# Eight weight jobs of the first gate moved from the dense attention loop into the Fourier stage

## The chip, the cores and the metric

The kernel runs on one core of a Trainium2 chip. The metric is the device time of one execution in microseconds (us). Its engines are named as the profile names them: PE (TensorE, matmuls; PEld its weight loads), DVE (VectorE), ACT (ScalarE), POOL (GpSimd), SP (SyncE, which issues the weight transfers here).

## What is computed

The reference is a network of two layers of one kind and a third block of another kind, on 512 tokens of width 1024. The change touches the mixers of the two layers alone:

```python
u = rmsnorm(x, g_mix[l])
p = u @ w_in[l]                       # 1024 Fourier columns, 3 x 384, 2 x 512, 512
y_a = fourier_mix(a_in) @ w_br_a[l]   # real part of a 2-D DFT over tokens and the 128 channels of each of 8 groups
y_b = dilated_mixture(qb, kb, vb, rel_bias[:, :6]) @ w_br_b[l]   # 3 pairs of heads, weighted by shares
y_c = diff_attention(qc, kc, vc, ...) @ w_br_c[l]                # 4 heads, a = p0 - lam * p1, 512 x 512 scores
gates = sigmoid(u @ w_gate[l] + b_gate[l]).reshape(..., 3, D)
merged = gates[0] * y_a + gates[1] * y_b + gates[2] * y_c
x = x + merged @ w_out[l]
```

## The kernel before, in words

All activations are held transposed: 128 channels of a tile on the partitions, 512 tokens along the free axis; 1024 channels are 8 tiles. Every product with a weight matrix is cut into **jobs**. A job is one 128 x 1024 slab of weights (512 KB, one row of `jobs` in DRAM) and gives one output tile of 128 x 512 in a PSUM bank. For precision each operand is split into a high part, rounded to fp32r, and a low part, so `product` (L429) issues three matmuls for each of 8 input tiles, 24 of 512 columns in all (L436 to L438), over `w_hi`, `w_lo` and the activations' `hi` and `lo`.

Weights pass through two slots, `s` = 0 and 1. SP loads `raw[:, s]` (L388) when POOL has made the slot's previous `w_lo`; ACT's `pump(s)` (L942) copies `raw` to `w_hi` in two halves, the first as soon as the job before it in the slot is half done, the second when it is done; POOL makes `w_lo = raw - w_hi` (L401). All jobs of the program are in one list that `arrays_of` builds (L2124), and jobs with even places use slot 0. So the order of jobs on PE is the order in the list, and PE, ACT, DVE and the list have to agree. Job s gives bank `ps[s]`; DVE's `scaled` (L1460) reads it out times `rs`, the reciprocal norm, and signals `evac[s]`, for which the next job in the bank waits.

Each engine has its own program, in order, with semaphores between the engines; `Count` keeps the values. In a layer the mixers go: 18 jobs of `w_in`; three dilated groups with 12 jobs between their steps; `dilated_rows`; `fourier`; `mix_groups`; `dense`; 8 jobs of the two other branch products; 14 of the other gates; 8 of `w_out`.

**Fourier stage** (PE L467, ACT L1020, DVE L1502). For each of 8 groups PE does the transform along the channels of the next group (`along_channels`, L471, from the folded inputs in `pt`, into ps2 or ps3), for groups 1 to 4 the transposes of a value tile for the later dense stage (L487), and the transform along the tokens (L493 to L499) in two banks: p with the cosines (ps4 or ps0), q with the sines (ps5 or ps1). ACT copies z (L1028) and q (L1037); DVE combines p and q in four operations to y (L1537 to L1540), ACT makes `m_hi` of it (L1039) and DVE `m_lo` (L1544): the activations of the branch product with `w_br_a`. No weight job runs in this stage, since the banks 0 and 1 hold q and p. Beside it DVE computes the shares of the dilated groups on two partitions (`dilated_rows`, `dilated_shares`, L1580 to L1601), and ACT their exponential (`mix_exp`, L1066).

**mix_groups** (PE L570, DVE L1603). The shares are spread to 128 partitions by a matmul with `sel` (L574, ps7), once for each of three dilated groups, and DVE multiplies and adds to `pt[:, MIX]`. It stands ahead of the first logits on DVE, through `hf` and T5 as temporaries.

**Dense loop** (PE L578, ACT L1070, DVE L1614). Sixteen rounds u, each 128 queries of one head, in a pipeline that is two rounds deep. PE in round u: scores of round u+2 (L586, two matmuls of 64 rows into ps2 and ps3, after the logits have freed them), wait for the probabilities, four transposes (L599, ps4), **one job** (L602, L604), wait for ACT's copy of the transposed tile (L1084), four PV matmuls (L609, ps5). DVE: `probabilities(u)` (L1635 to L1638), then what belongs to a job, then `logits(u+2)` (two operations L1624, a reduction L1628), which waits for the transposes of round u, since it overwrites their source. ACT: the copy, the gate's function and pump, the exponentials of round u+2 (L1076), the copies of PV (L1093, L1094).

Even rounds run a job of the first gate (`u_hi`, slot 0), which DVE scales into T7 and ACT puts through the sigmoid (L1086); odd rounds one of `w_br_a` (`m_hi`, slot 1), and DVE multiplies gate and product into `pt[:, u // 2 - 1]` one round later (L1654). So the two kinds alternate in the list.

Of the kernel before, what the change touches and what calls it, by code (L numbers as in the profile page):

```python
# [10 lines left out]
ALU = mybir.AluOpType  # L11
# [4 lines left out]
P = 128  # L16
S = 512
D = 1024
# [195 lines left out]
def build(nc, jobs, x_in, small_in, mem_in, pos_in, rel_in, lam_in, dft_in, hot_in, eye_in, sel_in,  # L214
          window_in, chunk_in, swap_in, rows8_in, out):
    NJ = jobs.shape[0]
    with ExitStack() as ctx:
# [64 lines left out]
        OC = 8  # L282
        MIX = 12
        YB, YC = 8, 16
        dft_c, dft_s = tab[:, 0:P], tab[:, P:2 * P]
# [130 lines left out]
        def _(pe):  # L416
# [50 lines left out]
            def fourier():  # L467
# [13 lines left out]
                for g in range(8):  # L481
                    if g < 7:
                        along_channels(g + 1)
                    if 1 <= g <= 4:
                        pe.wait_ge(vt_done, c.take("vt_done"))
                        for r in range(4):
                            mm = pe.transpose(ps[6][:, r * P:r * P + P], pt[:, VC + g - 1, r * P:r * P + P], ident)  # L487
                        mm.then_inc(vt_full, c.up("vt_full"))
                    z = T[:, g % 2].rearrange("p (t n) -> p t n", t=4)
                    pe.wait_ge(z_act, c.now("z_act") - (1 if g < 7 else 0))  # L490
                    pe.wait_ge(y_done, c.take("y_done") - 1)
                    p, q = ps[4 if g % 2 == 0 else 0], ps[5 if g % 2 == 0 else 1]
                    pe.matmul(p[:, 0:EVEN], z[:, 0], cos_even, start=True, stop=False)  # L493
                    if g == 0:
                        pe.wait_ge(middle_copied, c.next("middle"))
                    pe.matmul(p[:, 0:EVEN], middle, middle_of[:, g], start=False, stop=True)
                    pe.matmul(p[:, EVEN:HALF], z[:, 1], cos_odd, start=True, stop=True)
                    pe.matmul(q[:, 0:EVEN], z[:, 2], sin_even, start=True, stop=True)
                    pe.matmul(q[:, EVEN:HALF], z[:, 3], sin_odd, start=True, stop=True).then_inc(pq_full, c.up("pq"))  # L499

# [68 lines left out]

            def mix_groups(first_scores):  # L570
                pe.wait_ge(mixw_done, c.next("mixw"))
                for g in range(3):
                    pe.wait_ge(wb_free, c.take("wb_free"))
                    pe.matmul(ps[7][:, :], sel[:, :], rows_m[:, g], start=True, stop=True).then_inc(wb_full, c.up("wb_full"))  # L574
                    if g == 0:
                        first_scores()

            def dense():  # L578
# [9 lines left out]

                mix_groups(lambda: scores(0))
                pe.wait_ge(vt_done, c.now("vt_done"))  # L590
                scores(1)
                for u in range(16):
# [7 lines left out]
                    mm.then_inc(tr_full, c.up("tr_full"))  # L600
                    if u % 2 == 0:
                        job(0, u_hi, u_lo)  # L602
                    else:
                        job(1, m_hi, m_lo, ready=(m_ready, c.now("m")) if u == 1 else None)  # L604
                    pe.wait_ge(tr_copied, c.now("tr_copied"))
# [329 lines left out]
        def _(act):  # L935
# [84 lines left out]
            def fourier():  # L1020
# [3 lines left out]
                for g in range(8):  # L1024
                    act.wait_ge(z_full, c.next("z_full"))
                    if g >= 2:
                        act.wait_ge(pq_full, c.now("pq"))
                    act.activation(T[:, g % 2], ps[2 + g % 2][:, :], ACT.Copy).then_inc(z_act, c.up("z_act"))  # L1028
                    if g == 2:
                        mix_exp()  # L1030
                    if g:
                        fourier_out(g - 1)
                fourier_out(7)

            def fourier_out(g):
                act.wait_ge(pq_full, c.next("pq"))
                act.activation(T[:, 4 + 2 * (g % 2), 0:HALF], ps[5 if g % 2 == 0 else 1][:, 0:HALF], ACT.Copy).then_inc(q_copied, c.up("q_copied"))  # L1037
                act.wait_ge(y_done, c.next("y_done"))
# [31 lines left out]
            def dense():  # L1070
# [11 lines left out]
                for u in range(16):  # L1082
                    act.wait_ge(tr_full, c.next("tr_full"))
                    act.activation(T[:, 4 + u % 2], ps[4][:, :], ACT.Copy).then_inc(tr_copied, c.up("tr_copied"))  # L1084
                    if u % 2:
                        gate(T[:, 7], T[:, 7], 0, ACT.Sigmoid, bgate(0, u // 2))  # L1086
                    pump(1 - u % 2)
                    if u % 2:
                        skip(1)
                    if u < 14:  # L1090
# [336 lines left out]
        def _(dve):  # L1427
# [74 lines left out]
            def fourier():  # L1502
                for g in range(8):
                    if g:
                        fourier_out(g - 1)
                    if g > 1:
# [4 lines left out]
                    if g == 1:  # L1511
                        dilated_rows()
                    if g >= 4:
                        dilated_shares(g - 4)
                fourier_out(7)
# [15 lines left out]
            def fourier_out(g):  # L1531
                dve.wait_ge(q_copied, c.next("q_copied"))
                c.up("pq")
                if g > 1:
                    dve.wait_ge(m_ready, c.now("m"))
                y, p, q = T[:, 7 if g % 2 == 0 else 3], ps[4 if g % 2 == 0 else 0], T[:, 4 + 2 * (g % 2)]
                dve.tensor_tensor(y[:, 0:HALF:2], p[:, 0:EVEN], q[:, 0:EVEN], ALU.subtract)  # L1537
                dve.tensor_tensor(y[:, S - 2:HALF - 1:-2], p[:, 1:P], q[:, 1:P], ALU.add)
                dve.tensor_tensor(y[:, 1:HALF - 1:2], p[:, EVEN:HALF], q[:, EVEN:HALF], ALU.subtract)
                dve.tensor_tensor(y[:, S - 1:HALF - 1:-2], p[:, EVEN:HALF], q[:, EVEN:HALF], ALU.add).then_inc(y_done, c.up("y_done"))  # L1540

# [60 lines left out]

            def mix_groups():  # L1603
                for g in range(3):
                    dve.wait_ge(wb_full, c.next("wb_full"))
                    dst = hf if g == 0 else T[:, 5]
                    dve.tensor_tensor(dst, pt[:, QB + g], ps[7][:, :], ALU.mult).then_inc(wb_free, c.up("wb_free"))
                    dve.wait_ge(wb_free, c.now("wb_free"))
                    if g == 1:
                        step(dve.tensor_tensor(hf, hf, T[:, 5], ALU.add))  # L1610
                    if g == 2:
                        step(dve.tensor_tensor(pt[:, MIX], hf, T[:, 5], ALU.add))

            def dense():  # L1614
# [28 lines left out]
                for u in range(17):  # L1643
                    if u < 16:
                        probabilities(u)
                        c.up("tr_full")
                    if u % 2:
                        if u > 1:
                            dve.wait_ge(evac[1], c.now("evac1"))
                        scaled(0, T[:, 7])  # L1650
                    elif u:
                        dve.wait_ge(silu_done, c.next("silu"))
                        dve.wait_ge(job_done[1], c.next("job1"))
                        dve.tensor_tensor(pt[:, u // 2 - 1], T[:, 7], ps[1][:, :], ALU.mult).then_inc(evac[1], c.up("evac1"))  # L1654
                    if u < 14:
# [14 lines left out]
            def mixers():  # L1670
# [17 lines left out]
                fourier()  # L1688
                mix_groups()
                dense()  # L1690
# [433 lines left out]
def arrays_of(i):  # L2124

    jobs = []
    for l in range(LAYERS):
# [3 lines left out]
        jobs += [weight_jobs(i["w_in"][l]), np.zeros((1, P, D), np.float32)]  # L2131
        jobs.append(np.stack([a[0], weight_jobs(i["w_br_a"][l])], 1).reshape(-1, P, D))
        gates = np.stack([a[1], a[2]], 1).reshape(-1, P, D)
# [59 lines left out]
```

## Time and profile before

| | |
|---|---|
| three runs, median | 3734.37 us |
| lowest, highest | 3733.26, 3742.38 us |
| the profiled execution, its own time | 3740.04 us |
| its span in the trace | 3738.3 us |
| mean granted clock of PE | 0.967 |
| PE busy | 3511.4 us, 94% of the span |
| DVE, ACT, POOL busy | 1597.6, 1380.8, 1481.7 us |
| DMA | 309.08 MB, mean 83 GB/s |

The span is the time from the first to the last instruction in the trace; the execution's own time is 1.7 us longer. All times of rows are us from the span's start, from this one execution. The granted clock is a share of full speed, 2.4 GHz; 0.50 is 1.2 GHz. A fp32 matmul shows as two instructions, and ends of matmuls are modelled, so I read distances between starts.

### The profile page before, as it was taken

Reading aid. Unit: us, or ns where it says so; the run is one execution under the profiler, and the core shown is the slowest. Engines: PE = TensorE matmul, PEld = TensorE weight load, DVE = VectorE, ACT = ScalarE, POOL = GpSimd, SP = SyncE. Lnnn points to the kernel's source line nnn. Section 1 sums busy time; section 2 is a strip of 40 time slices with the busy share of each in tenths; the row PEclk is TensorE's granted clock in tenths of the full one; section 3 lists DMA queues with packets and bytes.
Section 4 is the critical chain, followed back from the end, with each engine's and each line's share of the span. In section 5 each row is a group of like instructions: output and inputs, shape, how many; then the busy total and the mean of one; then the engine's idle time right before and its main releaser. Section 6 shows DMA issues by size and latency. Waiting matters only on the chain.

```text
span 3738.3 us, 50030 instructions
## 1 busy us (share of the span) xinstructions
PE 3511.4 (94%) x16516; PEld 2872.7 (77%) x16516; DVE 1597.6 (43%) x2302; ACT 1380.8 (37%) x2387; POOL 1481.7 (40%) x1124
## 2 busy tenths in 40 slices
PE   8999998999999999999989999998897987889997
PEld 6888885778888888878757888886677886558886
DVE  4223525644322432244275442324786665243224
ACT  4223323644322432242346342324463233233222
POOL 4445431354444554454213544444220024224443
PEclk9999998999999999999989999999998998989998
DMA  3223321222222222232112322222120012113222
GB/s 113 98 98 101 116 73 38 69 96 95 96 97 100 97 101 99 97 122 95 57 44 73 107 94 97 96 95 90 51 74 9 10 40 90 45 51 100 97 95 90
DMA packets 87302, 309.08 MB, mean 83 GB/s; under 512 B 9823, under 2 KB 11873, under 8 KB 87060
## 3 DMA queue, kind: packets, MB, share of 16 engines
q1 hardware_dynamic: 82512, 297.96, 23.8%
q10 hardware_dynamic: 4676, 9.62, 0.9%
q8 instruction: 70, 1.15, 0.1%
q14 instruction: 44, 0.36, 0.0%
HBM read 305.36 MB, written 2.17 MB: 82 GB/s over the span
## 4 chain that ended last, share of the span: by engine, by line
PE 88%; DVE 7%; ACT 2%; issue 2%; ACTq 0%; DMA 0%; POOL 0%; DVEq 0%; POOLq 0%; SPq 0%
PE ps L436 26%; PE ps L438 25%; PE ps L437 25%; PE ps L846 1%; PE ps L586 1%; PE ps L855 1%; PE ps L609 1%; PE ps L849 1%; PE ps L916 1%; PE ps L599 1%; PE ps L524 0%; PE ps L755 0%; PE ps L901 0%; DVE x L1733 0%; PE ps L734 0%
## 5 line engine op out<-in xcount | busy, mean ns | idle before, releaser
L401 POOL TENSOR_TENSOR w_lo<-raw,w_hi 128x512 fp32r<-128x512 f32 x1120 | 1481.5, 1328 | 2227.5 <-ACT w_hi L946 1754.3
L436 PE MATMUL ps<-u_hi,w_hi 128*128 128x512 f32 (+1 forms) x2990 | 1177.1, 394 | 36.2 <-DVE u_lo L1722 16.4
L437 PE MATMUL ps<-u_hi,w_lo 128*128 128x512 f32 (+1 forms) x2990 | 1158.0, 387 | 0.0
L438 PE MATMUL ps<-u_lo,w_hi 128*128 128x512 f32 (+1 forms) x2990 | 1157.7, 387 | 0.0
L436 PEld LDWEIGHTS ps<-u_hi,w_hi 128*128 128x128 f32 x2990 | 568.1, 190 | 165.1 <-issue 36.2
L437 PEld LDWEIGHTS ps<-u_hi,w_lo 128*128 128x128 f32 x2990 | 568.0, 190 | 115.4 <-issue 5.8
L438 PEld LDWEIGHTS ps<-u_lo,w_hi 128*128 128x128 f32 x2990 | 567.3, 190 | 114.4
L948 ACT ACTIVATE w_hi<-raw 128x512 fp32r<-128x512 f32 x560 | 352.4, 629 | 764.9 <-PE ps L438 764.3
L436 PE MATMUL ps<-m_hi,w_hi 128*128 128x512 f32 x1344 | 529.5, 394 | 14.9 <-DVE m_lo L1467 11.9
L946 ACT ACTIVATE w_hi<-raw 128x512 fp32r<-128x512 f32 x560 | 350.9, 627 | 514.6 <-PE ps L438 475.3
L437 PE MATMUL ps<-m_hi,w_lo 128*128 128x512 f32 x1344 | 524.9, 391 | 0.0
L438 PE MATMUL ps<-m_lo,w_hi 128*128 128x512 f32 x1344 | 524.8, 390 | 0.0
L1463 DVE TENSOR_TENSOR T<-ps,rs 128x512 f32<-128x512 f32 x284 | 196.2, 691 | 752.8 <-PE ps L438 750.2
L436 PEld LDWEIGHTS ps<-m_hi,w_hi 128*128 128x128 f32 x1344 | 253.7, 189 | 71.1 <-DVE m_lo L1467 9.8
L438 PEld LDWEIGHTS ps<-m_lo,w_hi 128*128 128x128 f32 x1344 | 253.4, 189 | 53.2
L437 PEld LDWEIGHTS ps<-m_hi,w_lo 128*128 128x128 f32 x1344 | 253.8, 189 | 52.2 <-issue 0.2
L1479 DVE SCALAR_TENSOR_TENSOR x<-ps,x 128x512 f32 x112 | 77.5, 692 | 342.6 <-PE ps L438 342.6
L1474 DVE TENSOR_TENSOR T<-T 128x512 f32<-128x512 f32 x110 | 181.6, 1651 | 18.7 <-DVE T L1463 16.0
L971 ACT ACTIVATE m_hi<-T 128x512 f32 (+1 forms) x130 | 82.1, 632 | 277.5 <-DVE T L1474 217.0
L1467 DVE TENSOR_TENSOR m_lo<-T,m_hi 128x512 f32 (+1 forms) x138 | 97.7, 708 | 128.7 <-ACT m_hi L971 116.2
L1463 DVE TENSOR_TENSOR pt<-ps,rs 128x512 f32<-128x512 f32 (+1 forms) x76 | 52.4, 690 | 223.5 <-PE ps L438 223.0
L966 ACT ACTIVATE T<-T 128x512 f32<-128x512 f32 x110 | 69.8, 634 | 20.4 <-DVE T L1463 10.6
(410 smaller groups left out, 2772.7 us busy)
## 6 DMA issues: line engine op xcount, KB each, us to landing
raw<-jobs SPq DMA_DIRECT2D x560, 512.0 KB, 3.3
tab<-vec_dram ACTq DMA_DIRECT2D x8, 448.0 KB, 5.1
x<-x_in SPq DMA_DIRECT2D x4, 512.0 KB, 7.2
out<-x SPq DMA_DIRECT2D x8, 256.0 KB, 2.0
tab<-dft_in ACTq DMA_DIRECT2D x2, 901.0 KB, 4.7
tab<-chunk_in ACTq DMA_DIRECT2D x1, 1024.0 KB, 4.9
tab<-mem_in ACTq DMA_DIRECT2D x4, 256.0 KB, 3.0
tab<-vec_dram ACTq DMA_DIRECT2D x4, 128.0 KB, 7.2
```

Source lines behind the costliest of these rows:

```text
L401: pool.tensor_tensor(w_lo[:, s, w], raw[:, s, w], w_hi[:, s, w].bitcast(F32), ALU.subtract).then_inc(lo_done[s], 1)
L436: pe.matmul(ps[bank][:, 0:n], w_hi[:, s, w], hi[:, k, 0:n], start=k == ks[0], stop=False)
L437: pe.matmul(ps[bank][:, 0:n], w_lo[:, s, w], hi[:, k, 0:n], start=False, stop=False)
L438: last = pe.matmul(ps[bank][:, 0:n], w_hi[:, s, w], lo[:, k, 0:n], start=False, stop=k == ks[-1])
L946: act.activation(w_hi[:, s, half_of(0)], raw[:, s, half_of(0)], ACT.Copy).then_inc(hi_done[s], 1)
L948: act.activation(w_hi[:, s, half_of(1)], raw[:, s, half_of(1)], ACT.Copy).then_inc(hi_done[s], 1)
L966: act.activation(dst, src, func, bias=bias).then_inc(silu_done, c.up("silu"))
L971: act.activation(tile(m_hi, k), hf if src is None else src, ACT.Copy).then_inc(m_hi_done, c.up("m_hi"))
L1463: dve.tensor_tensor(dst, ps[s][:, :], rs[:, :], ALU.mult).then_inc(evac[s], c.up(f"evac{s}"))
L1467: dve.tensor_tensor(tile(m_lo, k), hf if src is None else src, tile(m_hi, k).bitcast(F32), ALU.subtract).then_inc(m_ready, c.up("m"))
L1474: dve.tensor_tensor(hf, sg, ur, ALU.mult).then_inc(h_done, c.up("h"))
L1479: dve.scalar_tensor_tensor(out=tile(x, k), in0=ps[s][:, :], scalar=scale, in1=tile(x, k), op0=ALU.mult, op1=ALU.add).then_inc(evac[s], c.u ...
```

## The change

The eight jobs of the first gate run in the Fourier stage, one a group, in the slots 0 and 1 in turn, ahead of the group's own transform along the tokens. To free banks 0 and 1 for them, p and q of a group share one bank, `ps[4 + g % 2]`: the sine of column 0, which is zero, and of the middle column are left out, so that 257 + 255 columns fit in 512; DVE copies columns 0 and 256 of y from p by themselves, which makes five operations of four. DVE scales a gate tile into `pt[:, g]` one group later, and ACT applies the sigmoid in place. The shares' step moves one group forward on DVE. The three `sel` matmuls are spread: the first in Fourier group 7, the others in the dense rounds 0 and 1, DVE's part in rounds 0 to 2 with temporaries in `pt`. In the dense loop only odd rounds have a job, of `w_br_a`, in the slots in turn, and its product with the gate is taken in the following even round. The list of jobs has the eight of the gate first and then the eight of the branch.

```diff
@@ PE, fourier
                     if g < 7:
                         along_channels(g + 1)
+                    job(g % 2, u_hi, u_lo)
+                    if g == 7:
+                        share_out(0)
                     if 1 <= g <= 4:
...
-                    p, q = ps[4 if g % 2 == 0 else 0], ps[5 if g % 2 == 0 else 1]
+                    p = ps[4 + g % 2]
...
-                    pe.matmul(q[:, 0:EVEN], z[:, 2], sin_even, start=True, stop=True)
-                    pe.matmul(q[:, EVEN:HALF], z[:, 3], sin_odd, start=True, stop=True).then_inc(pq_full, c.up("pq"))
+                    pe.matmul(p[:, HALF:HALF + P - 1], z[:, 2], sin_even[:, 1:P], start=True, stop=True)
+                    pe.matmul(p[:, HALF + P - 1:S], z[:, 3], sin_odd, start=True, stop=True).then_inc(pq_full, c.up("pq"))
@@ PE, shares
-            def mix_groups(first_scores):
-                pe.wait_ge(mixw_done, c.next("mixw"))
-                for g in range(3):
-                    pe.wait_ge(wb_free, c.take("wb_free"))
-                    pe.matmul(ps[7][:, :], sel[:, :], rows_m[:, g], start=True, stop=True).then_inc(wb_full, c.up("wb_full"))
-                    if g == 0:
-                        first_scores()
+            def share_out(g):
+                if g == 0:
+                    pe.wait_ge(mixw_done, c.next("mixw"))
+                pe.wait_ge(wb_free, c.take("wb_free"))
+                pe.matmul(ps[7][:, :], sel[:, :], rows_m[:, g], start=True, stop=True).then_inc(wb_full, c.up("wb_full"))
@@ PE, dense
-                mix_groups(lambda: scores(0))
+                scores(0)
...
-                    if u % 2 == 0:
-                        job(0, u_hi, u_lo)
-                    else:
-                        job(1, m_hi, m_lo, ready=(m_ready, c.now("m")) if u == 1 else None)
+                    if u < 2:
+                        share_out(1 + u)
+                    if u % 2:
+                        job(u // 2 % 2, m_hi, m_lo, ready=(m_ready, c.now("m")) if u == 1 else None)
@@ ACT, fourier
                     if g:
                         fourier_out(g - 1)
+                    pump(1 - g % 2)
+                    if g:
+                        gate(pt[:, g - 1], pt[:, g - 1], (g - 1) % 2, ACT.Sigmoid, bgate(0, g - 1))
                 fourier_out(7)
+                gate(pt[:, 7], pt[:, 7], 1, ACT.Sigmoid, bgate(0, 7))
@@ ACT, dense
                     if u % 2:
-                        gate(T[:, 7], T[:, 7], 0, ACT.Sigmoid, bgate(0, u // 2))
-                    pump(1 - u % 2)
-                    if u % 2:
-                        skip(1)
+                        pump(1 - u // 2 % 2)
+                        skip(u // 2 % 2)
@@ DVE, fourier
                     if g:
+                        scaled((g - 1) % 2, pt[:, g - 1])
                         fourier_out(g - 1)
...
-                    if g >= 4:
-                        dilated_shares(g - 4)
+                    if 3 <= g < 7:
+                        dilated_shares(g - 3)
+                scaled(1, pt[:, 7])
                 fourier_out(7)
@@ DVE, fourier_out
+                dve.tensor_copy(y[:, 0:HALF:2 * P], p[:, 0:EVEN:P])
+                dve.tensor_tensor(y[:, 2:HALF - 1:2], p[:, 1:P], q[:, 0:P - 1], ALU.subtract)
...
@@ DVE, shares (mix_groups ahead of dense() is gone)
+            def mix_group(g):
+                dve.wait_ge(wb_full, c.next("wb_full"))
+                dst = pt[:, MIX_PART + (g > 0)]
+                dve.tensor_tensor(dst, pt[:, QB + g], ps[7][:, :], ALU.mult).then_inc(wb_free, c.up("wb_free"))
+                dve.wait_ge(wb_free, c.now("wb_free"))
+                if g:
+                    step(dve.tensor_tensor(pt[:, MIX_PART if g == 1 else MIX], pt[:, MIX_PART], dst, ALU.add))
@@ DVE, dense
-                    if u % 2:
-                        if u > 1:
-                            dve.wait_ge(evac[1], c.now("evac1"))
-                        scaled(0, T[:, 7])
-                    elif u:
+                    if u < 3:
+                        mix_group(u)
+                    if u and u % 2 == 0:
+                        m = u // 2 - 1
                         dve.wait_ge(silu_done, c.next("silu"))
-                        dve.wait_ge(job_done[1], c.next("job1"))
-                        dve.tensor_tensor(pt[:, u // 2 - 1], T[:, 7], ps[1][:, :], ALU.mult).then_inc(evac[1], c.up("evac1"))
+                        dve.wait_ge(job_done[m % 2], c.next(f"job{m % 2}"))
+                        dve.tensor_tensor(pt[:, m], pt[:, m], ps[m % 2][:, :], ALU.mult).then_inc(evac[m % 2], c.up(f"evac{m % 2}"))
```

## Rows read from the trace of the kernel before

**Rows 1.** The page: the chain that ended last, by engine

```profile
PE 88%; DVE 7%; ACT 2%; issue 2%; ACTq 0%; DMA 0%; POOL 0%; DVEq 0%; POOLq 0%; SPq 0%
```

**Rows 2.** Busy time in windows: length, then PE, PEld, DVE, ACT, POOL, PEclk, DMA, GB/s

```profile
588.00:622.00 34.00, 24.87 (x163) 21.54 (x164) 24.54 (x52) 13.58 (x27) 0.00 (x0) 0.86 0.00 1
622.00:650.00 28.00, 22.10 (x64) 10.75 (x63) 16.25 (x25) 6.91 (x19) 2.54 (x2) 0.63 0.22 68
650.00:700.00 50.00, 50.00 (x251) 38.55 (x250) 35.28 (x51) 33.58 (x72) 16.69 (x12) 1.00 0.19 64
```

**Rows 3.** Timeline, Fourier stage: start, length, engine, line; in brackets idle before and releaser

```profile
592.13 0.39 PE L493 MATMUL ps<-tab,T 128*128 128x129 f32 x2
...
594.96 0.39 PE L493 MATMUL ps<-tab,T 128*128 128x129 f32 x2
...
596.47 1.06 PE L471 MATMUL ps<-tab,pt 128*128 128x128 f32 x8
...
597.36 0.60 PE L487 MATMUL ps<-eye,pt 128*128 128x128 f32 x4
...
597.79 0.39 PE L493 MATMUL ps<-tab,T 128*128 128x129 f32 x2
...
602.89 0.66 PE L487 MATMUL ps<-eye,pt 128*128 128x128 f32 x4 [2.54 <-DVE pt L1510]
...
616.16 0.64 PE L499 MATMUL ps<-tab,T 128*128 128x128 f32 x2
```

**Rows 4.** Timeline, head of the dense loop

```profile
621.40 2.06 PE L574 MATMUL ps<-pt,sel 2*128 2x512 f32 x2 [4.61 <-DVE T L1540]
...
631.95 1.29 DVE L1624 SCALAR_TENSOR_TENSOR T<-ps,tab 128x512 f32<-128x512 f32 x2
...
636.77 2.08 PE L586 MATMUL ps<-pt 64*128 64x512 f32 x4 [1.39 <-DVE T L1624]
...
637.88 0.15 DVE L1635 RECIPROCAL stats<-stats 128x2 f32<-128x2 f32 x1
...
639.60 1.11 PE L599 MATMUL ps<-eye,T 128*128 128x128 f32 x4 [0.75 <-DVE T L1638]
```

**Rows 5.** Timeline, one steady round of the dense loop

```profile
657.12 0.66 PE L599 MATMUL ps<-eye,T 128*128 128x128 f32 x4
657.53 0.48 PE L436 MATMUL ps<-u_hi,w_hi 128*128 128x512 f32 x1
...
657.91 1.29 DVE L1624 SCALAR_TENSOR_TENSOR T<-ps,tab 128x512 f32<-128x512 f32 x2 [1.88 <-PE ps L599]
...
660.37 0.16 DVE L1635 RECIPROCAL stats<-stats 128x2 f32<-128x2 f32 x1
...
663.09 1.05 PE L609 MATMUL ps<-pt,T 128*128 128x128 f32 x8
...
665.13 0.66 PE L599 MATMUL ps<-eye,T 128*128 128x128 f32 x4
```

**Rows 6.** Timeline, the last transposes of the dense loop, first layer

```profile
758.94 0.60 PE L599 MATMUL ps<-eye,T 128*128 128x128 f32 x4
```

**Rows 7.** The page's costliest groups: POOL's `w_lo` and ACT's 128x512 copy to `w_hi`

```profile
L401 POOL TENSOR_TENSOR w_lo<-raw,w_hi 128x512 fp32r<-128x512 f32 x1120 | 1481.5, 1328 | 2227.5 <-ACT w_hi L946 1754.3
...
L948 ACT ACTIVATE w_hi<-raw 128x512 fp32r<-128x512 f32 x560 | 352.4, 629 | 764.9 <-PE ps L438 764.3
```

**Rows 8.** Windows of PE alone: length, busy time (instructions), PEclk, DMA, GB/s

```profile
581.50:584.80 3.30, 2.22 (x17) 1.00 0.43 146
...
598.50:601.90 3.40, 1.85 (x15) 1.00 0.00 0
...
615.60:642.80 27.20, 16.69 (x34) 0.50 0.17 51
...
3206.00:3212.80 6.80, 4.53 (x20) 1.00 0.00 0
...
3250.70:3254.00 3.30, 2.71 (x9) 0.50 0.48 159
```

More of the change, by code:

```diff
@@ L283, in build @@
         MIX = 12
+        MIX_PART = 14
         YB, YC = 8, 16
@@ L1032, in fourier @@
                         fourier_out(g - 1)
+                    pump(1 - g % 2)
+                    if g:
+                        gate(pt[:, g - 1], pt[:, g - 1], (g - 1) % 2, ACT.Sigmoid, bgate(0, g - 1))
                 fourier_out(7)
+                gate(pt[:, 7], pt[:, 7], 1, ACT.Sigmoid, bgate(0, 7))
             def fourier_out(g):
                 act.wait_ge(pq_full, c.next("pq"))
-                act.activation(T[:, 4 + 2 * (g % 2), 0:HALF], ps[5 if g % 2 == 0 else 1][:, 0:HALF], ACT.Copy).then_inc(q_copied, c.up("q_copied"))
+                act.activation(T[:, 4 + 2 * (g % 2), 0:S - HALF], ps[4 + g % 2][:, HALF:S], ACT.Copy).then_inc(q_copied, c.up("q_copied"))
                 act.wait_ge(y_done, c.next("y_done"))
@@ L1535, in fourier_out @@
                     dve.wait_ge(m_ready, c.now("m"))
[L1536 to L1540, printed above, removed]
+                y, p, q = T[:, 7 if g % 2 == 0 else 3], ps[4 + g % 2], T[:, 4 + 2 * (g % 2)]
+                dve.tensor_copy(y[:, 0:HALF:2 * P], p[:, 0:EVEN:P])
+                dve.tensor_tensor(y[:, 2:HALF - 1:2], p[:, 1:P], q[:, 0:P - 1], ALU.subtract)
+                dve.tensor_tensor(y[:, S - 2:HALF - 1:-2], p[:, 1:P], q[:, 0:P - 1], ALU.add)
+                dve.tensor_tensor(y[:, 1:HALF - 1:2], p[:, EVEN:HALF], q[:, P - 1:S - HALF], ALU.subtract)
+                dve.tensor_tensor(y[:, S - 1:HALF - 1:-2], p[:, EVEN:HALF], q[:, P - 1:S - HALF], ALU.add).then_inc(y_done, c.up("y_done"))
             def fourier_low(g):
@@ L1601, in dilated_shares @@
                     dve.tensor_tensor(rows_m, rows_m, pt[0:2, 29:30, :].broadcast_to([2, 3, S]), ALU.mult).then_inc(mixw_done, c.up("mixw"))
[L1603 to L1612, printed above, removed]
+            def mix_group(g):
[5 more added lines that the diff above has]
+                    step(dve.tensor_tensor(pt[:, MIX_PART if g == 1 else MIX], pt[:, MIX_PART], dst, ALU.add))
             def dense():
@@ L1688, in mixers @@
                 fourier()
-                mix_groups()
                 dense()
@@ L2131, in arrays_of @@
         jobs += [weight_jobs(i["w_in"][l]), np.zeros((1, P, D), np.float32)]
-        jobs.append(np.stack([a[0], weight_jobs(i["w_br_a"][l])], 1).reshape(-1, P, D))
+        jobs += [a[0], weight_jobs(i["w_br_a"][l])]
         gates = np.stack([a[1], a[2]], 1).reshape(-1, P, D)
```

## The prediction

> **What bounds the kernel now.** I read the chain that ended last first: 88% of it is TensorE, mostly the three lines of `product` [rows 1]. The changed code runs twice (two layers), in two stages only, so their windows come next. The Fourier stage and the head of the dense loop are the loose places: PE is busy 24.87 of 34 us, then 22.10 of 28 us at a mean clock of 0.63, while from 650 on it is busy all the time at 1.00 [rows 2]. A job moved forward goes to where PE has room, and is taken from where it has none. The question is what bounds the place that it leaves.
>
> In the Fourier stage a group that waits for nothing repeats after 2.83 us: 1.51 for L493 to L499, 0.89 for L471, 0.43 for L487. From 592.13 that makes 8 x 1.51 + 6 x 0.89 + 4 x 0.43 = 19.1 us of work; it took until 616.8, so only some **5.6 us per layer** of stall can be filled there, the largest gap being 2.54 us for DVE [rows 3].
>
> The head of the dense loop is the larger hole, 22.8 us from 616.8 to the first transposes at 639.60. PE waits 4.61 us for `fourier_out(7)`, which stands behind `dilated_shares` on DVE; two `sel` matmuls take 2.06 us at half clock; DVE starts the first logits only after `mix_groups`, at 631.95; 7.65 us later come the transposes [rows 4].
>
> The steady dense round repeats after 8.01 us and is all PE: transposes 0.41, job 5.56, PV and scores 2.04 [rows 5].
>
> **The change, part by part, for one layer.**
>
> *Eight jobs into the Fourier stage.* Each group gets 5.5 us more of PE, and PE becomes the bound: 592.1 + 19.1 + 8 x 5.5 + one `sel` matmul at full clock (1.0, half of what row 621.40 has for two) = **656.2**. Its cover: ACT in each group does five 128x512 operations and a short one, each about 0.63, with a DVE turn between that I estimate at 1.1 (four operations in 0.9 and the new fifth, 0.2), then POOL two of 1.33 [rows 7]. A job's weights are so ready 6.5 us or less after the previous group ended, where they are wanted after 8.3 + 0.9, so 2.7 us of slack. The third group is tighter: `mix_exp` waits there for row work on DVE. I bound that from 0 to 1 us and take 0.5. The new DVE operation counts once, behind the last group. SP issues the same 512 KB transfers, one per 8.3 us and not per 8.0. Sum: end of Fourier **656.7**, 39.9 later, for 44 us of jobs taken in.
>
> *Head of the dense loop.* `mix_groups` no longer stands between. After the last matmul: q copy and five DVE operations 1.6, two `fourier_low` with the wait on m_hi 1.5, then logits(0); from there 7.65 as before [rows 4]: **10.75**. The bias DMAs (ACT, three issues) and a change of activation table lie beside DVE's 7.65; unhidden they would be at most about 2 us. The first transposes come at 667.45 against 639.60: **+27.9**.
>
> *The dense loop.* Odd rounds keep a job and stay at 8.01. Even rounds lose it, and what is late next is DVE. Its chain: transposes to the start of the logits 0.79, two logits and the reduction 2.46 until the reciprocal [rows 5], from there to the next transposes 1.72 (637.88 to 639.60, PE waiting) [rows 4]. So **4.97**, where PE has 2.45 of work. The gate product (one DVE operation, 0.69) and POOL's work fall into the odd round. A pair drops from 16.02 to 12.98: 3.04 won for each 5.5 removed. Nearest bounds of the light round are 2.45 (PE alone) and 5.7 (the product not hidden); I take the chain, since each link has its row. The last even round has no logits, PE waits for the copy alone: 2.3.
>
> Rounds 0 and 1 are at half clock: PE waits much of the 10.75 us before them, and where it did so before, the clock was 0.50 from 615.6 to 642.8 [rows 8]. Round 0 with `share_out(1)`: transposes 0.9, `sel` 2.0, PV 1.8, scores 2.08 [rows 4] = 6.8. Round 1: 2.9 until its job, 5.5, PV and scores 2.0, and a job that starts at half rate. Before, the first job ran so for some 2.5 us; I take 4, worth 2, since less goes before it: 12.4.
>
> From first to last transposes: 6.8 + 12.4 + 6 x 4.97 + 5 x 8.01 + 6.95 (a round without scores, 8.01 - 1.06) + 2.3 = **98.3**. Before: 758.94 - 639.60 = 119.3 [rows 4, 6]. Won: **21.0**.
>
> Behind the last transposes nothing differs: a job, two gate jobs, the tail with oT.
>
> **Sum.** +27.9 - 21.0 = +6.9 per layer, **+13.8 us** for both: the change fills 5.6 us of stall and takes 12 out of the head, but opens 2.5 us in each of six light rounds, one more in the last of them, and 7 in the two cold ones. The profiled execution took 3740.04 us; the median of three is 3734.37, 5.7 lower. On that median: **3748**, +0.37%. About 0.3% (11 us) is what a measurement of this kernel can tell from no change.
>
> **Rivals.**
>
> *A. The clock falls in the light rounds.* For it: in the cross-attention stage, where PE also waits between jobs, it is 0.50 again at 3250.7. Against: at 598.5 PE was busy 1.85 of 3.4 us and at 3206 4.53 of 6.8, both at 1.00 [rows 8]. A light round and the PV and scores before it have gaps of 0.9 and 1.5 in 7 us, so it is near the edge. A fall like that one (3.3 us at 0.50), if it lies in a job, costs half its length, 1.7. In half of the 12 light rounds: +10, 3758; in all: +20, 3768. The Trainium skill ("TensorE: Matmul & The Clock Gate", section "HAM oscillation — how this bites in real kernels") describes bursts of matmuls that are each followed by a wait, so that the clock is gated in every turn and each burst starts cold; by that rule the upper price would hold. No dense round of before has such a wait, so the trace doesn't settle it for this loop.
>
> *B. The clock stays up through the head.* Then round 0 takes 5 and not 6.8, round 1 9.0 and not 12.4, the head 0.4 less: -5.6 per layer, 3748 - 11 = 3737, not slower. For it: from 581.5 to 584.8 PE had only small matmuls and the clock stayed at 1.00. Against: 615.6 on [rows 8].
>
> *C. The Fourier stage isn't bound by PE.* If the weights come late in every group, ACT's queue being held by m_hi, which waits for DVE, the jobs wait: 1 us in 14 groups is +14, 3762. Against: the slack of 2.7 us.
>
> *D. Light rounds follow PE, not DVE: faster.* If the chain were overlapped, a light round would come near PE's 2.45; at 3.5 it is -1.5 x 12 = -18, 3730. It is faster than before from a chain below 3.8 us on (13.8 / 12 = 1.15 less). Against: L1624 started only when the transposes were done (0.79), and DVE has the logits ahead of the next probabilities in its order.
>
> That the change doesn't do what it says has next to no weight: jobs, products and matmuls are the same in number, only their places move.
>
> **Numbers.** Forecast 0.56, A 0.17, B 0.13, C 0.08, D 0.06. The forecast's own range is 3742 to 3754 (cold job 1 to 6 us, light chain within 0.2), so about 0.2 of its 0.56 lies within 0.3%. Faster: D and a little of B, 0.08. Slower: 0.36 of the forecast, A, and half of C: 0.57. Same: the rest, 0.35. The range goes down to below B and takes in A by half and C: 3734 to 3763.
>
> **What would show it.** Right: the last L499 near 656.5; first transposes some 11 us later; dense rounds alternating 8.0 and 5.0, the light one ending with a PE wait for DVE L1638; PEclk 1.00 from round 2 on; last transposes 7 us later than before. Wrong: light rounds under 4.5 or over 5.5; half clock inside the steady loop; jobs in the Fourier stage that wait for POOL; no fall of the clock ahead of round 0.

## The result, and the profile after

| | before | after |
|---|---|---|
| median of six runs | 3736.01 us | 3753.01 us |
| lowest, highest | 3732.11, 3742.38 us | 3752.39, 3754.82 us |
| profiled execution, its span | 3740.04, 3738.3 us | 3754.82, 3753.0 us |
| mean granted clock | 0.967 | 0.968 |

The ratio is 1.0046, with a 95% interval of 1.0034 to 1.0058: **17 us slower**, where 13.8 were forecast.

For each layer I read three marks from the timeline: the start of the Fourier stage (the `middle` matmul, L478 before and L479 after), the first transposes of the dense loop and the last ones. "The stages" are below the time from the first of these marks to the last; the head is the part from the last Fourier matmul to the first transposes; a dense round with a job is called heavy, one without a job light. Times in us from the stage's start:

| | first transposes | last transposes |
|---|---|---|
| before, layers 1 and 2 | 51.2, 51.3 | 170.5, 170.9 |
| forecast | 79.0 | 177.3 |
| after, layers 1 and 2 | 78.6, 79.5 | 173.9, 177.7 |

Outside the two stages the span holds 3396.9 us before and 3401.4 after. So 10.2 of the 14.8 us between the two profiled executions lie in the stages, and 4.5 outside, which the forecast had at nothing.

The Fourier stage in the timeline of the kernel after (start, length, engine, line), PE alone, two groups:

```profile
599.03 0.38 PE L497 MATMUL ps<-tab,T 128*128 128x129 f32 x2
...
600.52 1.06 PE L472 MATMUL ps<-tab,pt 128*128 128x128 f32 x8
...
607.35 0.39 PE L497 MATMUL ps<-tab,T 128*128 128x129 f32 x2
```

A group with its job and its value transposes now takes 8.32 us, where it took 2.83 [rows 3], and no row of PE in the eight groups shows a wait: PE now bounds the stage. The windows of the kernel after show that the clock was full there, and what became of it afterwards (length, PE busy, PEclk, DMA share, GB/s):

```profile
593.20:657.60 64.40, 64.40 (x342) 1.00 0.19 65
...
661.50:675.10 13.60, 10.86 (x26) 0.50 0.27 78
675.20:764.00 88.80, 75.41 (x391) 1.00 0.13 42
...
1938.20:1961.90 23.70, 19.12 (x43) 0.50 0.20 59
```

The third row answers to the last of [rows 2]: there PE was busy for 50.00 of 50 us, here for 75.41 of 88.80, at the same full clock. Those 13.4 idle us are the light rounds' (2.1 us of waits in each of six, and 0.97 in the last).

The head and the first rounds, timeline of the kernel after, first layer:

```profile
657.54 0.39 PE L503 MATMUL ps<-tab,T 128*128 128x128 f32 x2
...
659.38 1.13 PE L588 MATMUL ps<-pt 64*128 64x512 f32 x4 [1.46 <-DVE T L1547]
...
660.75 1.29 DVE L1628 SCALAR_TENSOR_TENSOR T<-ps,tab 128x512 f32<-128x512 f32 x2
...
668.39 1.11 PE L601 MATMUL ps<-eye,T 128*128 128x128 f32 x4 [0.75 <-DVE T L1642]
669.43 2.07 PE L578 MATMUL ps<-pt,sel 2*128 2x512 f32 x2
...
671.43 2.08 PE L611 MATMUL ps<-pt,T 128*128 128x128 f32 x8
...
675.32 0.66 PE L601 MATMUL ps<-eye,T 128*128 128x128 f32 x4
```

It is the chain of the forecast: DVE starts the first logits 3.2 us after the last Fourier matmul, and 7.64 later come the transposes, as before [rows 4]. Round 0 takes 6.93 us, with its `sel` matmul at 2.0 us and PV at 2.0; PE waits for nothing in it.

One light and one heavy round, the same timeline:

```profile
684.57 0.66 PE L601 MATMUL ps<-eye,T 128*128 128x128 f32 x4
...
685.37 1.29 DVE L1628 SCALAR_TENSOR_TENSOR T<-ps,tab 128x512 f32<-128x512 f32 x2 [1.95 <-PE ps L601]
685.99 1.15 PE L611 MATMUL ps<-pt,T 128*128 128x128 f32 x8 [0.76 <-ACT T L1090]
...
687.83 0.16 DVE L1639 RECIPROCAL stats<-stats 128x2 f32<-128x2 f32 x1
...
689.54 0.66 PE L601 MATMUL ps<-eye,T 128*128 128x128 f32 x4 [1.34 <-DVE T L1642]
...
697.55 0.66 PE L601 MATMUL ps<-eye,T 128*128 128x128 f32 x4
```

The light round is 4.97 us, the heavy one 8.01. PE waits twice in the light one, 0.76 for ACT's copy and 1.34 for L1642, the last of the four operations on the probabilities. All light rounds from 2 to 12 take 4.93 to 4.97, in both layers.

In the second layer round 1 takes 12.01 us and not 9.26. Timeline of the kernel after, second layer:

```profile
1939.17 2.08 PE L588 MATMUL ps<-pt 64*128 64x512 f32 x4 [1.45 <-DVE T L1547]
...
1956.07 1.11 PE L601 MATMUL ps<-eye,T 128*128 128x128 f32 x4
1957.11 2.07 PE L578 MATMUL ps<-pt,sel 2*128 2x512 f32 x2
...
1966.04 1.05 PE L611 MATMUL ps<-pt,T 128*128 128x128 f32 x8
...
1968.08 0.66 PE L601 MATMUL ps<-eye,T 128*128 128x128 f32 x4
```

There the half clock lasts until 1961.9, into the job; in the first layer it ended at 675.1, before the job began, and even the `sel` matmul of round 1 ran fast. The first row is that of the first scores: 2.08 us at half clock, where the first layer's took 1.13.

### The profile page after: what moved, and what is told of

Read it like the earlier page. It is cut to its first block, busy times and chain, and to the rows that moved or that the text cites. A ratio compares the mean times of both kernels' runs of the same rounds, so it can differ in the third digit from the quotient of the medians.

```text
span 3753.0 us, 50000 instructions
## 1 busy us (share of the span) xinstructions
PE 3519.1 (94%) x16516; PEld 2876.2 (77%) x16516; DVE 1584.3 (42%) x2318; ACT 1351.4 (36%) x2365; POOL 1477.1 (39%) x1124
## 4 chain that ended last, share of the span: by engine, by line
PE 88%; DVE 7%; ACT 2%; issue 2%; ACTq 0%; POOL 0%; DMA 0%; DVEq 0%; POOLq 0%; SPq 0%
PE ps L437 26%; PE ps L439 25%; PE ps L438 25%; PE ps L848 1%; PE ps L857 1%; PE ps L588 1%; PE ps L851 1%; PE ps L611 1%; PE ps L601 1%; PE ps L918 1%; PE ps L472 0%; PE ps L528 0%; PE ps L757 0%; PE ps L903 0%; DVE x L1735 0%
## 5 line engine op out<-in xcount | busy, mean ns | idle before, releaser
L950 ACT ACTIVATE w_hi<-raw 128x512 fp32r<-128x512 f32 x560 | 352.4, 629 | 764.7 <-PE ps L439 764.0
L437 PE MATMUL ps<-m_hi,w_hi 128*128 128x512 f32 x1344 | 531.0, 395 | 14.8 <-DVE m_lo L1471 11.9
L1467 DVE TENSOR_TENSOR T<-ps,rs 128x512 f32<-128x512 f32 x268 | 185.1, 691 | 736.7 <-PE ps L439 734.1
L1467 DVE TENSOR_TENSOR pt<-ps,rs 128x512 f32<-128x512 f32 (+1 forms) x92 | 63.4, 689 | 276.8 <-PE ps L439 276.0
```

What stands on the lines that cost most here:

```text
L437: pe.matmul(ps[bank][:, 0:n], w_hi[:, s, w], hi[:, k, 0:n], start=k == ks[0], stop=False)
L950: act.activation(w_hi[:, s, half_of(1)], raw[:, s, half_of(1)], ACT.Copy).then_inc(hi_done[s], 1)
L1467: dve.tensor_tensor(dst, ps[s][:, :], rs[:, :], ALU.mult).then_inc(evac[s], c.up(f"evac{s}"))
```

## The experiments

The kernels below were run against the kernel before on the same chip; the ratio is always to it. Most of them place the 16 jobs of the two stages by a table, so that one edit says where a gate job stands. `F` are the Fourier groups that have one, `R` the dense rounds; these edits are given in short, not as code.

**Jobs back in the loop, the rest of the change kept.**

```diff
-    F = 0..7, R = none, first sel matmul in group 7
+    F = none, R = 0, 2, .. 14, first sel matmul behind the second scores
```

> This kernel is the changed one with all eight gate jobs back in the even dense rounds; the one bank for p and q and the spread `sel` matmuls stay (the first now after the second scores). My theory: what the change gains lies in the head (no mixing ahead of the first logits, DVE not behind at the last Fourier group), what it loses lies in the light rounds. So here the gain stands alone: first transposes some 12 us earlier than before, rounds 0 and 1 some 3 us longer in all for their `sel` matmuls, about -9 us per layer, 3718 against 3736. All later rounds 8.01 us. Rival: the spread of the shares and the fifth DVE operation cost as much as they save, and the slowdown comes from them; then 3736 or above.

Measured: 3736.69 us, ratio 0.9997 (0.9988 to 1.0007). My number missed by 19 us. The rival's number held, and the first half of its claim: the rest of the change costs about what it saves. Its second half, that the slowdown comes from there, fell: with the jobs back no slowdown is left. The stages took 167.7 and 167.8 us, 3 less than before and not 9: the first transposes came at 44.0, 7.2 earlier than before and not 12, because the Fourier stage is 4.3 us longer; and rounds 0 and 1 took 12.65 and 9.25 us where they were 9.5 and 8.0. Why the Fourier stage is longer shows in its timeline:

```profile
612.31 3.33 DVE L1649 RECIPROCAL pt<-pt 2x512 f32<-2x512 f32 x1
...
617.35 0.58 ACT L1052 ACTIVATE T<-ps 128x512 f32<-128x512 f32 x1
...
617.98 0.80 PE L512 MATMUL ps<-tab,T 128*128 128x129 f32 x2 [3.22 <-ACT T L1052]
```

The reciprocal holds DVE, behind it wait y and `m_hi` of that group, behind these ACT's copy of z, and PE waits 3.22 us for that. The changed kernel has the same operations in the same order, hidden by jobs of 5.5 us. So the jobs cover more in the Fourier stage than the 5.6 us of stall seen before, and a part of what the head gains is only moved there from the Fourier stage.

**More PE work in the light rounds.**

```diff
+                    if u % 2 and 3 <= u < 14:
+                        pe.matmul(ps[6][:, :], ident, x[:, 1], start=True, stop=True)
...
+                    elif 2 <= u < 14:
+                        pe.matmul(ps[6][:, :], ident, x[:, 0], start=True, stop=True)
```

> The changed kernel with two more fp32 matmuls of 512 columns (identity times x, into a bank that nobody reads, 0.85 us each) in each light round from 2 to 12, 1.7 us more PE work in each of six rounds of two layers. My theory: DVE's chain bounds the light rounds and PE has 2.4 us to spare, so they stay at 4.95 us and the time at 3753, within 3. Rival (PE, or its clock, sets the light rounds): 12 x 1.7 = 20 us more, 3773.

Measured: 3755.03 us, ratio 1.0045 (1.0031 to 1.0059), as my theory had it and not the rival's 3773. Timeline of this kernel, a light round:

```profile
685.73 1.02 PE L610 MATMUL ps<-x,eye 128*128 128x512 f32 x2
...
688.80 1.13 PE L598 MATMUL ps<-x,eye 128*128 128x512 f32 x2
...
690.20 0.66 PE L603 MATMUL ps<-eye,T 128*128 128x128 f32 x4 [0.28 <-DVE T L1646]
```

The two matmuls take 2 us more of PE, PE's wait for the probabilities shrinks from 1.34 to 0.28, and the light round stays at 4.96. PE's work doesn't bound it.

**A shorter chain on DVE.**

```diff
-                    dve.tensor_reduce(stats[...], T[:, 2 * b:2 * b + 2], AX.X, ALU.max, negate=True)
+                    n = S if u % 2 else S // 2
+                    dve.tensor_reduce(stats[...], T[:, 2 * b:2 * b + 2, 0:n], AX.X, ALU.max, negate=True)
```

> The changed kernel with the row maximum of even rounds' logits taken over half of the keys (256 and not 512 of each map; the softmax is the same up to rounding, since the shift cancels). That takes 0.6 us out of DVE's chain of a light round and touches nothing on PE. My theory: light rounds 2 to 12 fall from 4.95 to 4.35, 12 x 0.6 = -7, 3746. Rival (something other than DVE's chain bounds them): 3753, unchanged.

Measured: 3748.19 us, ratio 1.0029 (1.0014 to 1.0043). Timeline of this kernel:

```profile
699.53 0.66 PE L601 MATMUL ps<-eye,T 128*128 128x128 f32 x4
...
701.62 0.69 DVE L1633 TENSOR_REDUCE stats<-T 128x2 f32<-128x512 f32 x1
...
703.93 0.66 PE L601 MATMUL ps<-eye,T 128*128 128x128 f32 x4 [0.77 <-DVE T L1643]
```

The reduction takes 0.69 for 1.22, and each light round 4.40 for 4.93: 0.53 out of DVE, 0.53 out of the round. With the run before it this settles what bounds a light round. The medians alone wouldn't: this kernel's interval and that of the changed one (1.0034 to 1.0058) overlap, and the reading rests on the rows.

**A job in the head, behind the second scores.**

```diff
-    F = 0..7
+    F = 0..6, and one gate job behind scores(1)
```

> The changed kernel with one of the eight gate jobs (that of group 7) moved from the Fourier stage to behind the second scores, where PE waits for DVE. Fourier stage 5.5 us shorter; head 1.4 longer, since the job ends a little behind the first probabilities; and if the job keeps the clock at 1.00, rounds 0 and 1 lose their cold part, 2 and 2 to 5 us. My theory: -5.5 + 1.4 - 3.6 = -7.7 per layer, 3738. Rival 1, the clock falls all the same: -4 per layer, 3745. Rival 2, the job only changes places and the head grows by its whole length: 3753.

Measured: 3743.20 us, ratio 1.0016 (1.0006 to 1.0026), between my number and the first rival. The stages took 170.3 us each. The Fourier stage is 5.5 shorter, as said, round 0 4.94 and round 1 9.28, but the head is 14.5 us, 3 to 4 longer than in the changed kernel and not 1.4. Windows of this kernel, PE alone:

```profile
652.50:654.70 2.20, 0.75 (x4) 0.99 0.00 0
654.70:661.50 6.80, 5.35 (x12) 0.50 0.84 274
```

The clock fell ahead of the job: its first 2.7 us ran at half rate, and the second scores too. The clock was back before the job ended, so the rounds ran at the full one, and the job bore the cold part itself.

**PE kept busy through the head.**

```diff
+                pe.matmul(ps[6][:, :], ident, x[:, 4], start=True, stop=True)   # ahead of scores(0)
                 scores(0)
+                pe.matmul(ps[6][:, :], ident, x[:, 0], start=True, stop=True)
                 scores(1)
+                pe.matmul(ps[6][:, :], ident, x[:, 1], start=True, stop=True)
...
+                    for k in range(2 if u == 0 else 1 if u == 1 else 0):
+                        pe.matmul(ps[6][:, :], ident, x[:, 2 + k], start=True, stop=True)
```

> The changed kernel with six fp32 matmuls (identity times x, into a bank that nobody reads, 0.85 us each at full clock) in PE's idle time of the head: one ahead of the first scores, one behind the first, one behind the second, two ahead of the first transposes, one in round 0. They compute nothing. My theory: the cold part of rounds 0 and 1 is the clock's doing; with PE kept busy, round 0 takes 5 us (6.93 and 7.06 in the changed kernel) and round 1 takes 9.3 in both layers (9.26 and 12.01), the head at most 0.4 less, so 2 to 7 us less per layer, in all about -8, 3745. Rival: the rounds are long from their `sel` matmuls and mixing on DVE, whatever the clock: 3753, rounds 6.9 and 9 to 12 us.

Measured: 3742.83 us, ratio 1.0017 (1.0007 to 1.0026). Windows of this kernel from the end of the Fourier stage, first and second layer:

```profile
656.00:675.00 19.00, 17.50 (x62) 1.00 0.24 74
1929.00:1948.00 19.00, 17.49 (x62) 1.00 0.25 74
```

and of the kernel after, the same 19 us in the first layer:

```profile
657.00:676.00 19.00, 13.82 (x42) 0.64 0.29 88
```

Six matmuls that compute nothing keep the clock at 1.00 through the head. The head takes 9.84 us in both layers (0.9 and 1.7 less, where I had allowed 0.4), round 0 4.91 and 4.93 us, round 1 9.26 and 9.29; the stages 171.0 and 171.1 us, against 173.9 and 177.7. That is 9.6 us less in the two stages, and 10 in the medians (3753.01 and 3742.83, of different sets of runs). The same rounds with the same `sel` matmuls and mixing are short at full clock, so what made them long is the clock.

**The changed kernel again, and the kernel before twice, for traces.**

> The changed kernel once more, for a second trace. In the first, the two changed stages took 10 us more than before, yet the median grew by 17. Between the stages the runs so far differ too (3394 to 3403 us), and with them the number of clock falls of 3.4 us in the dilated stage (5 to 10 in two layers). My theory: each such fall costs some 1.5 us and their number depends on where the stage begins against the clock's own grid; a second trace with n falls shows about 3387 + 1.55 n us outside the two stages. Rival: the time outside is fixed by the change itself, 3401 again whatever n is.

> The kernel before, for a second trace. Its two changed stages should take 170.5 to 170.9 us again (PE-bound rounds, little chance in them), and the time outside them 3387 + 1.55 n us for n falls of the clock in the dilated stages, 5 or 6 of them. If the growth of 17 us against 10 in the stages comes from more falls in the changed kernel, this one shows fewer than 8. Rival: the number is chance alone and as often 9 or 10 here.

> The kernel before, a third trace, with the same expectations: stages 170.5 to 170.9, fewer than 8 falls, outside 3394 to 3398 us. Rival: 8 or more falls.

> The changed kernel, a third trace. Stages 173.9 to 179 us each, by how much of the head and of round 1 runs at half clock. If the rest of the 17 us is in more falls in the dilated stages, 8 or more of them and 3400 us or more outside the two stages (the first trace had 9 and 3401, the second 5 and 3397). Rival: the number is chance alone; then it may be 5 or 6 and 3397 here, and the rest of the growth stays open.

The changed kernel has 3754.41 us here, ratio 1.0046 (1.0029 to 1.0063), as the first time. The traces:

| trace | its time | stages | outside | falls in the dilated stages |
|---|---|---|---|---|
| before, first | 3740.04 | 170.5 + 170.9 | 3396.9 | 4 + 2 |
| before, second | 3742.53 | 170.6 + 170.8 | 3399.4 | 4 + 4 |
| before, third | 3741.77 | 170.7 + 170.8 | 3398.5 | 5 + 2 |
| after, first | 3754.82 | 173.9 + 177.7 | 3401.4 | 5 + 4 |
| after, second | 3750.49 | 174.0 + 177.7 | 3397.1 | 5 + 0 |
| after, third | 3764.15 | 179.2 + 179.2 | 3403.9 | 5 + 5 |

A fall here is a stretch of 3.4 us at 0.50 that begins within 80 us ahead of a Fourier stage or with its first matmuls; the last column has those of the first layer and of the second. The stages of before repeat within 0.2 us; those of after spread over 5, and the spread lies between the last Fourier matmul and the end of round 1. (The one exception is the second layer of the second trace: its Fourier stage, with no fall at its start, is 1.6 us shorter, and its round 1 is 1.6 us longer than in the first trace.) Windows of the third trace of the kernel after:

```profile
659.20:686.40 27.20, 22.32 (x50) 0.50 0.23 71
...
1946.00:1973.20 27.20, 22.36 (x50) 0.50 0.22 71
```

27.2 us at half clock in both layers, against 13.6 and 23.7 in the first trace; round 1 then takes 13.5 us. This trace comes from another chip than the second one, but the second one's chip also gave times from 3749.62 to 3766.19 us in five runs. The mean over three traces: stages 353.9 after and 341.4 before, +12.5; outside 3400.8 and 3398.2, +2.6. The kernel before had 6, 8 and 7 falls, so my "fewer than 8" for it held once and failed once; the changed one had 9, 5 and 10, the last as I expected. Three traces each don't show a difference in the number. My 3387 + 1.55 n us outside for n falls hit the second trace of before (3399.4) and missed the second of after by 2.3 us (3394.8 for 3397.1); its rival, 3401 whatever n is, fell with that trace.

Where the time outside differs can be read more closely. Behind the second layer's stages it is 1705.6 to 1706.3 us in all six traces. Ahead of the first Fourier stage it is 587.9 and 588.4 us with 4 falls and 589.8 to 590.8 with 5, whichever the kernel. Between the first layer's last transposes and the second layer's Fourier stage it is 1102.2 us with 2 falls (before, first and third), 1105.6 with 4 (before, second), and in the kernel after 1105.9 with 4, 1100.6 with none and 1107.6 with 5. With the same 4 falls the two kernels are 0.3 us apart, so what the changed kernel has more outside its stages goes with the number of falls and not with other work there. Why the number varies is open.

**Jobs only where PE waits for DVE.**

```diff
-    F = 0..7, R = none, first sel matmul in group 7
+    F = 2, 5, one job behind scores(0), R = 2, 4, .. 10, first sel matmul behind the second scores
```

> Jobs only where PE waits for DVE: two gate jobs in the Fourier stage (group 2, beside the row work of the shares; group 5, beside the reciprocal), one behind the first scores, five back in the dense rounds 2 to 10; the first `sel` matmul behind the second scores. By my theory a job costs its 5.5 us wherever PE is the bound, and a round without one costs 2.5 us of idle PE, so the best place is where PE stands already. Fourier stage 35.5 us from its start, first transposes at 49, dense 5 + 9 + 9 x 8.01 + 8.01 + 5 + 6.9 + 2.6 = 108.5: 157.5 per layer against 170.7 before and 173.9 and 177.7 in the changed kernel, 3736 - 26 = 3710. Rival (the jobs are only shifted, and the head or DVE gives the time back): 3730 or above.

```diff
-    F = 0..7, R = none, first sel matmul in group 7
+    F = 2, 5, R = 2, 4, .. 12, first sel matmul behind the second scores
```

> As the kernel with a job in the head, but that job back in round 12: two gate jobs in the Fourier stage, six in the rounds 2 to 12. Head idle and cold again: first transposes at 47, rounds 0 and 1 6.9 and 11. By my theory 162.7 per layer, 3736 - 16 = 3720, so the job in the head is worth some 5 us per layer (its idle time filled and the clock kept). Rival (the head's idle time is worth nothing): the same time for both kernels within 3 us.

Measured: 3730.05 us, ratio 0.9976 (0.9966 to 0.9985), and 3720.07 us, ratio 0.9949 (0.9933 to 0.9966). The second number held, the first missed by 20 us, and its rival (3730 or above) came true. The stages take 161.8 and 161.7 us in the first kernel, 161.1 and 161.3 in the second. Two jobs in the Fourier stage lengthen it to 35.6 us from 28, so that 11 us of jobs cost 7.7. Against the kernel with all jobs back, which shares the new order on DVE, they cost 3.3 (35.6 for 32.3).

The second kernel's gain has another half: its light rounds are 0 and 14, and these give more than the others. Against the kernel with all jobs back round 0 falls from 12.65 to 7.06 us and round 14, which has no logits behind it, from 6.82 to 2.58: 9.8 us in all, where two steady rounds would give 6.1.

The job in the head is worth less than nothing: the kernel with it is 10 us slower than its sister, where I had some 5 us per layer in its favour and the rival the same time within 3 us. Timeline of the kernel with it, PE alone:

```profile
627.17 1.93 PE L603 MATMUL ps<-pt 64*128 64x512 f32 x4 [1.50 <-DVE T L1590]
...
635.52 1.13 PE L603 MATMUL ps<-pt 64*128 64x512 f32 x4
...
640.87 1.01 PE L619 MATMUL ps<-eye,T 128*128 128x128 f32 x4 [1.70 <-DVE T L1685]
```

The second scores come 8.35 us after the first, where they come 3.45 after it in the kernel without this job, and DVE's order has the second logits ahead of the first probabilities: the job delays the chain that the head consists of. First transposes at 51.1 for 47.0, 4 us later, and the light round 12 gives 3.1 back. Its stages sum to 1.2 us more than its sister's, and 4 more lie outside (10 falls for 7), so of the 10 us between the two medians I can place about half.

**Both findings together.** The kernel of the ratio 0.9949 with five of the matmuls that compute nothing in its head.

> The kernel with two gate jobs in the Fourier stage and six in the dense rounds 2 to 12 (3720 us, stages of 161.1 and 161.3), and in its head the matmuls that compute nothing, five of them: one ahead of the first scores, one behind, two ahead of the first transposes, one ahead of the second. By my theory the cold part of rounds 0 and 1 (7.06 and 9.4 us) is left to win, as it was in the changed kernel: round 0 5 us, round 1 9.2, the head 0.4 less, so stages of 158.6 and 3715. Rival: with the clock down in that head for 17 us only, half of it idle, nothing is left, 3720.

Measured: **3713.75 us, ratio 0.9938 (0.9922 to 0.9955)**. Windows of this kernel:

```profile
585.50:588.90 3.40, 3.40 (x17) 0.50 0.00 0
588.90:766.30 177.40, 169.43 (x863) 1.00 0.19 62
```

Behind the first 3.4 us of the Fourier stage no half clock is left until the end of the dense loop, and the stages take 157.2 and 157.3 us (3715 and 158.6 expected). The kernel is 23 us faster than the kernel before and some 39 faster than the changed one, whose runs are of another set.

## Why the prediction was right

**The Fourier stage** was forecast to end at 68.3 us from its start; the last matmul was issued at 67.9 in both layers. PE-bound from the first group, as said. The half us for the tight third group wasn't there: its period is 8.31, like those of its neighbours. The stall that jobs can fill was read too small: it was measured between PE's rows of the kernel before, and didn't count what DVE's order would cost after the shares' step had moved, the 4.3 us of the first experiment. In the changed kernel it made no difference, since jobs cover it. The row at 621.40 was misread as two `sel` matmuls: it is one, shown as two instructions, and the two others have rows of their own, 2.07 us each. The 1.0 us taken for one at full clock was right all the same (1.05 from its start to the next in group 7).

**The head**: 10.75 forecast, 10.7 and 11.6 measured. The clock of the first scores makes the 0.8 between the layers, 1.13 us at full clock and 2.08 at half.

**The light rounds**: 4.97 forecast from three rows of the kernel before, 4.93 to 4.98 measured, in all three traces of the changed kernel. The two experiments on them moved PE's work up by 2 us without effect and DVE's down by 0.53 with all of it. Rival D is excluded, by both.

**Rounds 0 and 1**: 6.8 and 12.4 forecast; 6.93 and 7.06, and then 9.26 and 12.01, and up to 13.6 in other traces. The second term was a guess in its size (the job cold for its first 4 us) and it carries most of the scatter: the job ran cold for 0 to 6 us. Rival B, a clock that stays up, didn't happen by itself in any trace; when it was made to happen, by six idle matmuls, the stages lost 9.6 us where its price had been put at 11.

**The last light round** was 2.56 for 2.3, PE waiting 0.97 for the copy, where it waits 0.76 in the others.

**Rival A**, a clock that falls in the light rounds, didn't happen: 1.00 from 675.2 to 764.0, with PE busy 85% of the time. The Trainium skill ("TensorE: Matmul & The Clock Gate", section "HAM oscillation — how this bites in real kernels") describes bursts that start cold because the clock was gated in the wait before each. In the head the clock fell among PE's waits and the scores behind them ran cold, 2.08 us for 1.13; the light rounds, with waits of 0.76 and 1.34 us, show no fall in any of the three traces. In that page's example PE waits for longer than it works. So it was in the head, where PE was busy for 1.16 of the 3.6 us ahead of the fall (657.9 to 661.5), and not in a light round, where it was busy for 2.87 of 4.97 (684.57 to 689.54); the forecast was wrong to say that its upper price would follow from this rule. **Rival C** is excluded by the Fourier groups of 8.3 us.

**The sum**: stages +13.8 forecast, +10.2 in the first trace, +10.3 in the second, +17.1 in the third. Outside the stages I had put nothing; there the traces of after have 2.6 us more on the mean, which goes with the number of falls, and whether that number is the change's doing is open. So of the 17 us by the medians some 12 lie in the stages, about 3 outside as far as three traces each can tell, and 2 aren't placed. That the total came within 3 us of the forecast is in part luck: in the first two traces the stages grew by 3.6 us less than forecast, nearly all of it in one layer's round 1 (9.26 for 12.4), and growth outside the stages, for which the forecast had no term, made up for it.

In words of the change: 88 us of jobs (16 x 5.5) left a place where PE was the bound, and brought only 3.04 us each in its steady rounds. They went to a place that hid 5 us of the 44 per layer: the Fourier stage grew by 40 us, 1 of them for the `sel` matmul.

## What to carry to other kernels

Work that moves out of a bound engine's loop saves only the distance to the next bound: read what a round would take without it from the chain of the second engine (here DVE, 4.97 us) and not from the engine's own sum (2.45). Move as many pieces as the receiving stage has gaps for, and no more, and take them from the rounds that give the most back: two jobs instead of eight, out of rounds 0 and 14, turned +0.5% into -0.5%. The runs don't part the two: no kernel took two jobs out of steady rounds. A gap that is itself a chain (the head) takes no job without lengthening: 3 to 4 us for a job of 5.5, less than in a stage that PE bounds and more than the 3.04 of a steady round.
Where PE idles ahead of a loop, a few matmuls that compute nothing can be worth more than moved work: 10 us here in the changed kernel.

## What the runs showed of the hardware that I had not expected

- Five or six fp32 matmuls that compute nothing, of 1 us each, spread over the head and round 0, held PE's clock at 2.4 GHz, where without them it ran at 1.2 GHz for 13.6 to 27.2 us. A `sel` matmul (2 rows, 512 columns, two instructions in the trace) took 2.07 us at half clock and 1.12 at full.
- In its first trace and layer the kernel before has a fall of the clock in the dilated stage once every 17.07 us (537.1, 554.1, 571.2, 588.3), the first of them where a group's scores have ended and its job begins. In all fourteen traces the Fourier stage starts within 0.5 us of such a fall (588.42 and 588.3, 1861.11 and 1861.4), except one, the second layer in the second trace of the kernel after, which has no fall at all. It looks as if the falls' own cost kept the groups in step with them; that isn't shown, and no run here was made for it.
- The changed kernel's round 1 took 9.25 to 13.57 us, by where the half clock ended. So one and the same stage took 173.9 to 179.2 us with the same code.
